# Routing stretch of a hybrid diffusion step: order of router logits, modulation chunks and list product, and who finishes four chunks

## The chip, the cores and the metric

The kernel runs on one core of one Trainium2 chip. The metric is device time in microseconds (us) of one execution; several runs are made and the median is taken. The engines are TensorE (PE), VectorE (DVE), ScalarE (ACT), GpSimd (POOL) and SyncE (SP), which issues most of the transfers. SPq, ACTq and POOLq are the instruction queues of those engines where they issue DMAs or do register work.

## The reference

Two trunk layers; each has a mixing sub-layer (pooling, neighbourhood attention, latent attention) and a channel sub-layer, a hierarchical mixture of experts. 128 context and 512 latent tokens share the weights; they differ in the conditioning vector. What matters here is the modulation and the routing:

```python
def modulation(cvec, w_mod, b_mod):
    m = (jax.nn.silu(cvec) @ w_mod + b_mod)[..., None, :]
    return jnp.split(m, 6, axis=-1)

def ada_norm(x, g, shift, scale):
    return rmsnorm(x, g) * (1.0 + scale) + shift

...
        xp = xp + gt1 * rmsnorm(y, g_post_mix[l])
        h = ada_norm(xp, g_pre_ffn[l], sh2, sc2)
        y = hier_moe(h, w_group_router[l], w_expert_router[l], w_exp_gate[l], w_exp_up[l], w_exp_down[l])
        xp = xp + gt2 * rmsnorm(y, g_post_ffn[l])
...
def hier_moe(h, w_group_router, w_expert_router, w1, w3, w2):
    ...
    gp = jax.nn.softmax((x @ w_group_router).astype(jnp.float32), axis=-1)
    g_w, g_idx = lax.top_k(gp, 1)
    el = (x @ w_expert_router).astype(jnp.float32).reshape(N, N_GROUPS, EXPERTS_PER_GROUP)
    el_g = jnp.take_along_axis(el, g_idx[:, :, None], axis=1)[:, 0]
    top_w, top_i = lax.top_k(jax.nn.softmax(el_g, axis=-1), TOP_K)
    top_w = top_w / jnp.sum(top_w, axis=-1, keepdims=True)
    expert_id = g_idx * EXPERTS_PER_GROUP + top_i
    ...
```

`D_MODEL` is 1024, there are 16 experts with a hidden width of 256, and everything is float32.

## The kernel before, in words

Each engine runs its own instruction stream over a loop of two layers and meets the others at semaphores. The 640 tokens are five tiles of 128. PE writes into three PSUM buffers, `pair0` to `pair2`, in turn: the list `plan_jobs` names every job of the layer in PE's order, and job i takes buffer i mod 3, so it waits until the reader of job i-3 has released it. The end of that list is written out by hand as `TAIL` (line 92).

The steps of `TAIL` are: `y` (output projection of one tile, 64 matmuls), `ht` (the tile of `h2`, the input of the experts, transposed by 8 PE transposes), `lg` (router logits of a tile: 16 matmul records of 128x20), `mod` (one chunk of 512 columns of the modulation: a weight chunk of 2 MB times the two conditioning vectors, 32 matmul records of 2x256), `cnt` (how many tokens before this one chose the same expert) and `list` (the token numbers of each block of 128 expert slots, 20 matmul records of 128x26). Chunks 6 and 7 are this layer's last gate `gt2`; 8 to 11 belong to the next layer's first norm. In this text mod 6 is the chunk with number 6, lg 4 the logits of tile 4.

The weight chunks lie in a ring of six units of 1 MB. A chunk of the modulation takes two, so mod 9 overwrites mod 6, and mod 10 mod 7. SP issues the loads in the order of `plan_chunks`: it waits until PE has read what lies there (line 605 and following), loads the weights, stores the finished rows of the chunk before the last one to `mod_rows` in DRAM (`store_mods`, which waits for `mod_row`), and loads the bias and gain rows `aux`. After mod 11 it waits for `blocks_ready` and for PE's mod 10, reads the expert number of the first block, and issues `w_gate`, `w_up` and `w_down` (lines 637 to 651).

DVE finishes every chunk: `mod_rows_of` (line 1021) adds the bias rows to the PSUM result and multiplies by the gain, two instructions each on 2 partitions by 256 columns. It also runs the routing, a chain of some 65 small instructions from line 1340 to 1414: maxima and one-hots, `chosen` for `cnt`, a wait for the exponentials of ACT (`routed_b`, line 1361), places and slots, `marks_ready` for `list` (line 1403), `blocks_ready` (line 1414). ACT copies each transposed tile out of PSUM, then waits until the rows of mod 6 and 7 are stored, issues the load of the broadcast gate `gb2` from them, and only then computes the two exponentials (lines 936 to 945).

POOL has nothing in this stretch until `list` has been read by DVE into `src_ids`. It then issues the indirect DMAs that gather 128 rows of `h2_rows` for each block of tokens. PE enters the loop over expert blocks with `gathered` (8 transposes), `up` (64 matmul records) and `down`. For the first block these need the gathered rows, the weights, and mod 9 to 11 read out of PSUM.

## Time and profile before

| what | value |
|---|---|
| median of 3 runs | 2143.77 us (2137.72 to 2143.83) |
| profiled execution | 2149.69 us, span 2147.9 us |
| PE busy | 1905.1 us, 89% of the span |
| DVE busy | 775.7 us, 36% |
| ACT busy | 564.6 us, 26% |
| POOL busy | 168.0 us, 8% |
| chain that ended last: PE | 79% |
| mean granted clock of TensorE | 0.949 |

The profile is one execution. Busy times alone do not tell where time can be saved: PE is the bound as a whole, and what the stretch of the change costs is read from PE's gaps there and from who ends them. In the rows of a timeline, the bracket at the end gives the time for which the engine stood idle before the row, and the work whose end released it. A granted clock of 1.00 is 2.4 GHz and 0.50 is 1.2 GHz.

### The profile page before, as it was taken

To read this page: it belongs to the slowest core of one execution; us is meant where nothing else is said; L and a number is where in the kernel's file an instruction comes from. 1 tells how busy PE (TensorE), PEld (TensorE's weight loads), DVE (VectorE), ACT (ScalarE), POOL (GpSimd) and SP (SyncE) were. 2 spreads that over 40 slices of the span, in tenths; PEclk is the share of its full clock that TensorE was granted. 3 is DMA by queue.
4 is the path that set the end of the run, shared out by engine and by line. 5 is a ranking of instruction groups with operands and counts; after the bars stand their busy time and mean duration, and the time that the engine had idled before them with its cause. 6 is when DMAs were issued, how large, how long until landed. Compare 5 with 4: busy or idle time off the path is not lost.

```text
span 2147.9 us, 30625 instructions
## 1 busy us (share of the span) xinstructions
PE 1905.1 (89%) x12556; PEld 1590.1 (74%) x12556; DVE 775.7 (36%) x1426; ACT 564.6 (26%) x909; POOL 168.0 (8%) x192
## 2 busy tenths in 40 slices
PE   3799898999999996999818998989999999979992
PEld 1698555779999884888708975556899998748881
DVE  1421556753222235111062226477423222341113
ACT  1311251652121120111152103526422111201113
POOL 0201510000000000011020033100000000000101
PEclk8799999999999997999958999999999999989996
DMA  9413352211132418999692123121113214389995
GB/s 338 149 62 82 121 168 79 99 59 60 60 99 74 171 70 309 347 351 361 236 312 84 50 63 140 40 79 60 60 60 99 74 64 177 132 299 359 355 342 206
DMA packets 197424, 340.94 MB, mean 159 GB/s; under 512 B 9948, under 2 KB 121964, under 8 KB 196972
## 3 DMA queue, kind: packets, MB, share of 16 engines
q1 hardware_dynamic: 167804, 266.16, 36.0%
q10 hardware_dynamic: 21728, 44.83, 5.9%
q0 software_dynamic: 7776, 28.32, 3.7%
q8 instruction: 85, 1.39, 0.3%
q14 instruction: 31, 0.25, 0.0%
HBM read 309.50 MB, written 41.30 MB: 163 GB/s over the span
## 4 chain that ended last, share of the span: by engine, by line
PE 79%; DVE 8%; DMA 5%; ACT 3%; issue 3%; SPq 1%; ACTq 1%; POOL 1%; POOLq 0%; DVEq 0%
PE pair L1592 70%; PE opair L1592 5%; PE pair L1638 3%; DVE mid L1178 1%; DMA ring<-in_w_mod 1%; DMA r<-mod_rows 1%; DMA r<-h_rows,ids 1%; DVE r L1434 1%; ACT r L959 1%; DVE mid L1190 1%; SPq L533 1%; ACT ysT_r L742 1%; ACTq L735 0%; DMA ysT<-in_mod_aux 0%; DVE mid L1307 0%
## 5 line engine op out<-in xcount | busy, mean ns | idle before, releaser
L1592 PEld LDWEIGHTS pair<-r,ring 128*128 128x128 f32 x2176 | 252.7, 195 | 18.7 <-issue 15.3
L1592 PE MATMUL pair<-r,ring 128*128 128x128 f32 x2176 | 253.2, 278 | 2.6 <-DVE r L1430 2.6
L1592 PE MATMUL pair<-hT_r,mid_r 128*128 128x320 f32 x768 | 237.3, 309 | 0.0
L1592 PE MATMUL pair<-r_r,ring_r 128*128 128x320 f32 x832 | 211.8, 309 | 2.2 <-DVE ring_r L1051 2.2
L1592 PE MATMUL pair<-ring,r 128*128 128x256 f32 (+1 forms) x776 | 204.7, 422 | 6.7 <-DVE r L1280 3.6
L1638 PE MATMUL pair<-cst,mid 128*128 128x128 f32 (+1 forms) x668 | 107.4, 300 | 113.6 <-DVE mid L1070 80.9
L1638 PEld LDWEIGHTS pair<-cst,mid 128*128 128x128 f32 (+1 forms) x668 | 82.0, 152 | 158.4 <-DVE mid L1070 85.0
L1592 PEld LDWEIGHTS pair<-ring,r 128*128 128x128 f32 x776 | 146.6, 191 | 53.2 <-issue 24.4
L1592 PE MATMUL pair<-ysT_r,mid_r 128*128 128x256 f32 (+1 forms) x768 | 170.5, 313 | 17.2 <-issue 17.2
L1592 PE MATMUL pair<-mid_r 128*128 128x320 f32 x576 | 178.9, 311 | 1.6 <-issue 1.6
L1592 PE MATMUL pair<-r_r,mid_r 128*128 128x256 f32 (+2 forms) x576 | 179.3, 311 | 0.0
L1592 PE MATMUL pair<-mid_r,ring_r 128*128 128x320 f32 x576 | 178.0, 309 | 0.0
L1592 PEld LDWEIGHTS pair<-r_r,ring_r 128*128 128x128 f32 x832 | 145.7, 188 | 2.8 <-DVE ring_r L1051 2.8
L1592 PEld LDWEIGHTS pair<-ysT_r,mid_r 128*128 128x128 f32 x768 | 131.9, 194 | 18.0 <-issue 18.0
L1592 PEld LDWEIGHTS pair<-hT_r,mid_r 128*128 128x128 f32 x768 | 144.2, 188 | 0.5 <-issue 0.5
L1276 DVE TENSOR_TENSOR r<-pair,r 128x640 f32<-128x640 f32 x48 | 39.5, 823 | 274.8 <-PE pair L1592 274.8
L1434 DVE TENSOR_TENSOR r<-r,pair 128x256 f32<-128x256 f32 x34 | 14.3, 421 | 343.4 <-ACT r L959 343.4
L1592 PE MATMUL pair<-r 96*128 96x320 f32 (+4 forms) x512 | 122.3, 431 | 6.4 <-issue 6.4
L881 ACT ACTIVATE r<-pair 128x640 f32<-128x640 f32 x48 | 33.8, 703 | 297.5 <-PE pair L1592 297.5
L1550 POOL COPY ids<-src_ids 128x1 uint32 x34 | 6.2, 184 | 1348.3 <-DVE src_ids L1418 529.2
L1592 PEld LDWEIGHTS pair<-r_r,mid_r 128*128 128x128 f32 x576 | 110.5, 192 | 0.0
L1592 PEld LDWEIGHTS pair<-mid_r 128*128 128x128 f32 x576 | 108.1, 188 | 3.0 <-issue 2.6
(247 smaller groups left out, 2919.1 us busy)
## 6 DMA issues: line engine op xcount, KB each, us to landing
ring<-in_w_mod SPq DMA_DIRECT2D x27, 2048.0 KB, 9.5
ring<-in_w_gate SPq DMA_DIRECT2D x34, 1024.0 KB, 7.0
ring<-in_w_up SPq DMA_DIRECT2D x34, 1024.0 KB, 12.2
ring<-in_w_down SPq DMA_DIRECT2D x34, 1024.0 KB, 10.9
ring<-in_w_in SPq DMA_DIRECT2D x24, 1024.0 KB, 7.3
expert_out<-r ACTq DMA_DIRECT2D x34, 512.0 KB, 7.4
ring<-in_w_in SPq DMA_DIRECT2D x8, 2048.0 KB, 13.6
ring<-in_w_branch SPq DMA_DIRECT2D x12, 1024.0 KB, 5.1
```

Of the source, the lines that this page charges most:

```text
L533: sp.dma_start(pro_w[i], w_mod[0, :, i * 512:(i + 1) * 512].rearrange("(k p) n -> p k n", p=P)).then_inc(pro_in[i], 16)
L742: ins = nc.scalar.copy(out, rows)
L881: nc.scalar.activation(sig[:, i % 2, :], ps[:, MID:MID + T], ACT.Sigmoid)\
L959: nc.scalar.activation(sil[:, s, :], pair[1][:, s * 512:s * 512 + FF], ACT.Silu).then_inc(sil_ready, 1)
L1178: V.tensor_tensor_reduce(by_columns(na_probs[i % 3][:, a * w:(a + 1) * w]), by_columns(ps[:, a * 512:a * 512 + w]), bias, -1.0, MOST, ALU. ...
L1190: ins = V.tensor_scalar(own, own, na_inv[i % 2][:, a:a + 1], None, ALU.mult)
L1276: ins = V.tensor_tensor(mergedT[:, m, :] if first else sig[:, i % 2, :], ps[:, MID:MID + T], sig[:, i % 2, :], ALU.mult)
L1434: V.tensor_tensor(hid[:, s, :], sil[:, s, :], pair[1][:, s * 512 + FF:s * 512 + 2 * FF], ALU.mult)\
L1550: G.tensor_copy(src_id[s], src_ids[:, ds(it * 2 + s, 1)]).then_inc(id_ready, 1)
L1592: return nc.tensor.matmul(out, lhsT, rhs, start=first, stop=last, skip_group_check=True)
L1638: last = nc.tensor.transpose(ps[0:s.shape[1], a:a + P], s, ident)
```

## The change

`TAIL` is reordered in two places: lg 4 goes ahead of mod 7, and `list` goes between mod 9 and mod 10. DVE reads the logits of tile t-2 right after the residual sum of tile t, and not at the end of the tile. Mod 6 to 9 are no longer finished by DVE: ACT copies them from PSUM to SBUF (`mod_evicted`), which frees the buffer, and POOL adds the bias and multiplies by the gain (`mod_rows_by_pool`). DVE finishes mod 10 and 11, both after its read of `list`. SP no longer stores rows ahead of a weight load of the modulation; the store behind the load remains. POOL reads the list once the rows of mod 0 to 9 are done.

```diff
-        ("lg", 2), ("ht", 3), ("mod", 6), ("lg", 3), ("ht", 4), ("mod", 7), ("lg", 4), ("mod", 8), ("cnt", 0),
-        ("mod", 9), ("mod", 10), ("list", 0), ("mod", 11)]
+        ("lg", 2), ("ht", 3), ("mod", 6), ("lg", 3), ("ht", 4), ("lg", 4), ("mod", 7), ("mod", 8), ("cnt", 0),
+        ("mod", 9), ("list", 0), ("mod", 10), ("mod", 11)]
...
+        def mod_rows_by_pool(pool, n):
+
+            pool.wait_ge(aux_in[n % 2], 16 * MT * (n // 2 + 1))
...
+            await_read(pool, ("mod", n))
+            for i in range(MT):
+                own = slice(32 * i, 32 * i + 2)
+                ins = nc.gpsimd.tensor_tensor(modst[n][own], modst[n][own], aux[n][own, 0:MW], ALU.add)
+            ins.then_inc(aux_added, 1)
+            pool.wait_ge(aux_added, n - N_IN + 1)
+            for i in range(MT):
+                own = slice(32 * i, 32 * i + 2)
+                nc.gpsimd.tensor_tensor(modst[n][own], modst[n][own], aux[n][own, MW:2 * MW], ALU.mult).then_inc(mod_row, 1)
+
+        def mod_evicted(act, n):
+
+            ps = await_job(act, ("mod", n))
+            if mod_before(n) is not None:
+                await_mod_stored(act, mod_before(n))
+            for i in range(MT):
+                own = slice(32 * i, 32 * i + 2)
+                ins = nc.scalar.copy(modst[n][own], ps[own, 0:MW])
+            ins.then_inc(freed[PAIR_OF[("mod", n)]], 1)
...
-                        if before[0] == "mod":
+                        if before[0] == "mod" and key[0] != "mod":
                             store_mods(before[1])
...
+                mod_evicted(act, N_IN)
                 tail_transposed(TT - 1)
-                await_mod_stored(act, N_IN)
-                await_mod_stored(act, N_IN + 1)
+                for n in range(N_IN + 1, N_IN + 3):
+                    mod_evicted(act, n)
+                for n in range(N_IN, N_IN + 2):
+                    await_mod_stored(act, n)
                 for g in range(2):
                     act.dma_start(gb2[:, g, :], mod_rows[g:g + 1, 5 * D:6 * D].partition_broadcast(P)).then_inc(gb_in, 16)
...
+                for n in range(N_IN + 3, NMOD - 2):
+                    mod_evicted(act, n)
                 act.wait_ge(rows_zeroed, 16 * (NB - spare + 1))
...
                     V.tensor_tensor(x2[:, t, :], x2[:, t, :], yb[:, t % 2, :], ALU.add).then_inc(x2_new, 1)
+                    if t >= 2:
+                        logits(t - 2)
                     inverse_root(t, 2 * t + 2)
...
-                    if t >= 2:
-                        logits(t - 2)
-                mod_rows_of(N_IN)
                 logits(TT - 2)
-                mod_rows_of(N_IN + 1)
                 logits(TT - 1)
...
-                mod_rows_of(N_IN + 2)
...
-                mod_rows_of(N_IN + 3)
-                mod_rows_of(N_IN + 4)
                 ps = await_job(dve, ("list", 0))
...
-                mod_rows_of(N_IN + 5)
+                dve.wait_ge(mod_row, MT * (NMOD - 2))
+                for n in (NMOD - 2, NMOD - 1):
+                    mod_rows_of(dve, V, n)
...
+                for n in range(N_IN, NMOD - 2):
+                    mod_rows_by_pool(pool, n)
+                pool.wait_ge(mod_row, MT * (NMOD - 2))
                 await_read(pool, ("list", 0))
```

On PE, at the end of a layer, from ht 3 to mod 11, the order before is this (`cst,ysT` is `ht`, `router_sb` is `lg`, `ring,cols` is `mod`, `small,cst` is `cnt`, `<-mid 128x26` is `list`):

```order
L1592 MATMUL pair2<-ring,cols 2x256 x16
L1592 MATMUL pair0<-router_sb,mid 128x20 x8
L1638 MATMUL pair1<-cst,ysT 128x128 x8
L1592 MATMUL pair2<-ring,cols 2x256 x16
L1592 MATMUL pair0<-router_sb,mid 128x20 x8
L1592 MATMUL pair1<-ring,cols 2x256 x16
L1592 MATMUL pair2<-small,cst 128x80 x2
L1592 MATMUL pair0<-ring,cols 2x256 x16
L1592 MATMUL pair1<-ring,cols 2x256 x16
L1592 MATMUL pair2<-mid 128x26 x10
L1592 MATMUL pair0<-ring,cols 2x256 x16
```

and now:

```order
L1628 MATMUL pair2<-ring,cols 2x256 x16
L1628 MATMUL pair0<-router_sb,mid 128x20 x8
L1674 MATMUL pair1<-cst,ysT 128x128 x8
L1628 MATMUL pair2<-router_sb,mid 128x20 x8
L1628 MATMUL pair0<-ring,cols 2x256 x16
L1628 MATMUL pair1<-ring,cols 2x256 x16
L1628 MATMUL pair2<-small,cst 128x80 x2
L1628 MATMUL pair0<-ring,cols 2x256 x16
L1628 MATMUL pair1<-mid 128x26 x10
L1628 MATMUL pair2<-ring,cols 2x256 x16
L1628 MATMUL pair0<-ring,cols 2x256 x16
```

Lg 4 has moved ahead of mod 7 and `list` ahead of mod 10; with them the PSUM buffers of lg 4, mod 7, `list` and mod 10 have changed.

On ACT, from the last transposed tiles to the exponentials (`r1<-` and `mid<-pair... 2x256` now are the copies of mod chunks, `hT<-mod_rows` is the load of `gb2`, of which the second row is left out), before:

```order
L915 COPY mid<-pair1 128x1024 [waits filled0,filled1]
L911 DMA h2_rows<-ysT 128x1024 [waits h2_ready]
L915 COPY mid<-pair1 128x1024 [waits filled0,filled1]
L940 DMA hT<-mod_rows 128x1024 [waits mod_stored1,mod_stored0]
L943 ACT_TABLE_LOAD
L943 ACTIVATE small<-small 128x20 [waits routed_a]
L945 ACTIVATE small<-small 128x5 [waits routed_a]
```

and now, with the first of the two copies of each chunk:

```order
L963 COPY mid<-pair1 128x1024 [waits filled0,filled1]
L570 COPY r1<-pair2 2x256 [waits filled2]
L959 DMA h2_rows<-ysT 128x1024 [waits h2_ready]
L963 COPY mid<-pair1 128x1024 [waits filled0,filled1]
L570 COPY mid<-pair0 2x256 [waits filled0]
L570 COPY r1<-pair1 2x256 [waits mod_stored0,filled1]
L991 DMA hT<-mod_rows 128x1024 [waits mod_stored1,mod_stored0]
L994 ACT_TABLE_LOAD
L994 ACTIVATE small<-small 128x20 [waits routed_a]
L996 ACTIVATE small<-small 128x5 [waits routed_a]
L570 COPY mid<-pair0 2x256 [waits mod_stored1,filled0]
```

The copies of mod 6, 7 and 8 now stand ahead of the load of `gb2` and of the exponentials; that of mod 9 stands behind them.

On DVE, from the last instruction of the routing to mod 11, the first of each two, before:

```order
L1414 CAST ids<-small 128x1 [waits dve_step]
L1030 SCALAR_TENSOR_TENSOR mid<-pair0,mid 2x256 [waits mod_stored1,aux_in1,filled0]
L1036 TENSOR_TENSOR mid<-mid 2x256 [waits freed0]
L1030 SCALAR_TENSOR_TENSOR r1<-pair1,mid 2x256 [waits mod_stored0,aux_in0,filled1]
L1036 TENSOR_TENSOR r1<-r1,mid 2x256 [waits freed1]
L1418 CAST src_ids<-pair2 128x26 [waits filled2]
L1030 SCALAR_TENSOR_TENSOR mid<-pair0,mid 2x256 [waits mod_stored1,aux_in1,filled0]
L1036 TENSOR_TENSOR mid<-mid 2x256 [waits freed0]
```

and now:

```order
L1447 CAST ids<-small 128x1 [waits dve_step]
L1449 CAST src_ids<-pair1 128x26 [waits filled1]
L535 SCALAR_TENSOR_TENSOR r1<-pair2,mid 2x256 [waits aux_in0,mod_stored0,filled2,mod_row]
L541 TENSOR_TENSOR r1<-r1,mid 2x256 [waits freed2]
L535 SCALAR_TENSOR_TENSOR mid<-pair0,mid 2x256 [waits mod_stored1,aux_in1,filled0]
L541 TENSOR_TENSOR mid<-mid 2x256 [waits freed0]
```

The read of `list` now directly follows the routing, and mod 10 follows it with a wait for all rows before.

## Rows read from the trace of the kernel before

**Rows 1.** Timeline of PE, both layers (start us, us, what)
```profile
806.69 2.13 PE L1592 MATMUL pair<-router_sb,mid 128*128 128x20 f32 x16 [2.10 <-DVE small L1300]
...
810.54 4.17 PE L1592 MATMUL pair<-ring,cols 128*2 128x256 f32 x32
...
816.53 3.62 PE L1592 MATMUL pair<-ring,cols 128*2 128x256 f32 x32
...
830.76 5.98 PE L1592 MATMUL pair<-ring,cols 128*2 128x256 f32 x32 [4.82 <-DMA ring<-in_w_mod]
836.68 2.41 PE L1592 MATMUL pair<-mid 128*128 128x26 f32 x20
839.02 3.62 PE L1592 MATMUL pair<-ring,cols 128*2 128x256 f32 x32
850.04 1.97 PE L1920 MATMUL pair<-cst,r 128*128 128x128 f32 x8 [7.40 <-DMA r<-h_rows,ids]
853.33 10.33 PE L1592 MATMUL pair<-r,ring 128*128 128x128 f32 x64 [1.32 <-DVE r L1430]
...
868.12 7.31 PE L1592 MATMUL pair<-r,ring 128*128 128x128 f32 x64
...
1917.51 9.07 PE L1592 MATMUL pair<-r,ring 128*128 128x128 f32 x64 [1.32 <-DVE r L1430]
```

**Rows 2.** Chain of waits, the first gather: start, us, what
```profile
841.62 8.38 DMA r<-h_rows,ids
```

**Rows 3.** Timeline of DVE, routing part
```profile
816.85 0.17 DVE L1340 TENSOR_REDUCE small<-small 128x5 f32<-128x20 f32 x1
...
821.43 0.24 DVE L1358 TENSOR_TENSOR small<-small 128x80 f32<-128x80 f32 x1
...
823.39 0.17 DVE L1362 TENSOR_REDUCE small<-small 128x5 f32<-128x20 f32 x1
...
832.26 0.50 DVE L1402 TENSOR_TENSOR mid<-mid,cst 128x130 f32<-128x130 f32 x2
```

**Rows 4.** Timeline of ACT, same stretch
```profile
803.91 1.01 ACT L915 COPY mid<-pair 128x1024 f32<-128x1024 f32 x1 [0.23 <-issue]
...
820.91 0.81 ACTq L940 DMA_DIRECT2D hT<-mod_rows  x2
821.75 1.28 ACT L943 ACT_TABLE_LOAD   x1 [10.10 <-DMA mod_rows<-mid]
```

**Rows 5.** Timeline of SP's queue
```profile
816.52 0.53 SPq L602 DMA_DIRECT2D mod_rows<-mid  x2
...
818.89 0.41 SPq L615 DMA_DIRECT2D ring<-in_w_mod  x1
...
837.34 1.47 SPq L632 DMA_DIRECT2D mid<-in_mod_aux  x2
841.09 0.41 SPq L647 DMA_DIRECT2D ring<-in_w_gate  x1
```

**Rows 6.** DMA issues 800.6 to 801, 841.5 to 842.1: KB each, us to landing
```profile
ring<-in_w_mod SPq DMA_DIRECT2D x1, 2048.0 KB, 14.7
...
ring<-in_w_up SPq DMA_DIRECT2D x1, 1024.0 KB, 10.8
```

**Rows 7.** Groups by line and form, ACT: busy us, mean ns
```profile
L755 ACT COPY r<-pair 128x256 f32<-128x256 f32 x8 | 3.0, 380 | 0.0
```

**Rows 8.** Groups by line and form, POOL
```profile
L1501 POOL TENSOR_TENSOR r_r<-hT,ysT_r 128x512 fp32r<-128x512 f32 x8 | 15.9, 2022 | 0.0
...
L1529 POOL TENSOR_TENSOR u_sb<-ysT,u_sb 128x656 f32<-128x656 f32 x8 | 12.7, 1591 | 0.6
...
L1527 POOL TENSOR_TENSOR ysT<-ysT,cst 128x8 f32<-128x8 f32 x32 | 5.7, 208 | 0.7
```

**Rows 9.** Stretches of 1 us: busy us by engine, PEclk, DMA share, GB/s
```profile
819.00:820.00 1.00, 1.00 (x12) 0.28 (x6) 0.85 (x5) 0.00 (x0) 0.00 (x0) 1.00 0.27 86
...
846.00:847.00 1.00, 0.00 (x0) 0.00 (x0) 0.00 (x0) 0.00 (x0) 0.00 (x0) 0.50 1.11 372
```

More of the change, by code:

```diff
@@ L1019, in link @@
                     dve.wait_ge(dve_step, steps[0])
-                def mod_rows_of(n):
-                    ps = await_job(dve, ("mod", n))
-                    dve.wait_ge(aux_in[n % 2], 16 * MT * (n // 2 + 1))
-                    if mod_before(n) is not None:
-                        await_mod_stored(dve, mod_before(n))
-                    one = 1.0 if MODS[n][0] // 2 in (1, 4) else 0.0
-                    for i in range(MT):
-                        own = slice(32 * i, 32 * i + 2)
-                        ins = V.scalar_tensor_tensor(out=modst[n][own], in0=ps[own, 0:MW], scalar=one, in1=aux[n][own, 0:MW],
-                                                     op0=ALU.add, op1=ALU.add)
-                    ins.then_inc(freed[PAIR_OF[("mod", n)]], 1)
-                    await_read(dve, ("mod", n))
-                    for i in range(MT):
-                        own = slice(32 * i, 32 * i + 2)
-                        V.tensor_tensor(modst[n][own], modst[n][own], aux[n][own, MW:2 * MW], ALU.mult).then_inc(mod_row, 1)
                 def split_low(i):
@@ L1155, in attend_context @@
                     V.tensor_tensor(c_probs, c_probs, by_head(c_inv), ALU.mult).then_inc(c_scaled, 1)
-                    mod_rows_of(n_mod)
+                    mod_rows_of(dve, V, n_mod)
                     await_job(dve, (kind + "c", 1))
@@ L1196, in neighbourhood @@
                         if i == 0:
-                            mod_rows_of(n_mod)
+                            mod_rows_of(dve, V, n_mod)
                             context_values("na", 1)
@@ L1232, in latent @@
                         if i == 0:
-                            mod_rows_of(n_mod)
+                            mod_rows_of(dve, V, n_mod)
                             context_values("ml", 2)
@@ L1237, in latent @@
                         if i == MOD_UNIT:
-                            mod_rows_of(N_ML)
+                            mod_rows_of(dve, V, N_ML)
                         if i % 3 == 2 and i // 3 < KD:
@@ L1266, in _ @@
                 split_low(N_WIN)
-                mod_rows_of(N_ML + 1)
+                mod_rows_of(dve, V, N_ML + 1)
                 await_mod_stored(dve, N_IN - 1)
```

22 lines of the change are left out of this document (added).

## The prediction

> **What bounds the kernel now.** I read the timeline of PE first. The change touches one stretch that occurs once in each of the two layers, from the last output tile to the first expert block, and PE's rows show what closes it. The reader is to see PE's gaps: it waits 2.1 us for DVE before the fourth router tile, 4.82 us for the weights of mod 10, and 7.40 us for the gathered rows before the first expert's transposes; from 853.33 on it runs on with no gap named [rows 1]. So a microsecond won or lost at the start of the first up-projection goes through one to one, and nothing else here counts. In what follows all times are those of the first layer; the second repeats it 1064 us later.
>
> Second, the chain of waits: the gather is issued at 841.62 and lands 8.38 us later [rows 2]. Third, DVE's timeline: routing starts at 816.85, `chs` is ready near 821.7, the part behind `routed_b` starts at 823.39, and the marks for the list product are done near 832.8 [rows 3]. ACT explains 823.39: its exponentials stand behind the load of `gb2`, which waits until the rows of mod 7 are stored; it issues that load at 820.91 and then loads a table for 1.28 us [rows 4]. Fourth, SP's queue: rows of mod 7 stored from 816.52, weights of mod 10 issued at 818.89, the last aux load at 837.34, and the first expert's `w_gate` at 841.09 [rows 5]. The landings of that queue: mod 8's weights 14.7 us after their issue at 800.7, and the first expert's `w_up` 10.8 us after its issue right behind `w_gate`'s, so at 852.4 [rows 6]. The gather path allows the first up-projection at 853.33 and the weights at 852.4: the two ends are within 1 us of each other, and a gain on the gather alone is worth almost nothing.
>
> **The change, part by part.**
>
> *The logits.* Before, lg 3 starts at 806.69, released by DVE's read of lg 2, which stood behind all of h2's work [rows 1]. Now that read comes before. What is late next is ACT's copy of ht 3, done at 804.9 [rows 4]: lg 3 starts near 805.0, ht 4 near 807.0, ACT copies it (1.0 us), lg 4 runs from 809.1 to 811.0. Mod 7 follows, 811.0 to 814.6 (3.62 us as mod 8 took). Routing on DVE then starts at 811.3 instead of 816.85, a lead of 5.6 us, and `chs` is there at 816.1. Mod 8 comes to its weights: 800.7 + 14.7 = 815.4, so it runs 815.4 to 819.0. The count product follows to 819.7 and mod 9 to about 824.5.
>
> *What becomes of the lead.* DVE still stops for `routed_b`, and ACT still issues `gb2` before its exponentials. So the release is the store of mod 7's rows, and these are now made by two engines. ACT: two copies, at 380 ns for 128x256 from PSUM [rows 7], so 0.76 us, ends at 815.4. POOL: four operations of 2x256. The trace has none of that size on POOL. Two-input additions and products there took 208 ns at 8 elements, 1591 ns at 656 (in place, as here) and 2022 ns at 512 in strided fp32r form [rows 8]. The line through the first two gives 0.208 + 248 x 2.13 ns = 0.74 us each; through the first and third 1.10 us each; the dearest bound is a whole 2.0 us each, the cheapest 0.2. I take 0.74, as these are plain in-place f32 rows: 3.0 us for four. Rows of mod 7 are then ready at 818.4 instead of 816.5: 1.9 us later, though PE delivers mod 7 at the same time as before (814.6). The store took from 816.52 to 820.9 before, and the two loads of DMA work in front of it are the same now; I take 821.4, with 820.9 and 822.8 as ends (the same 4.4 us from 818.4). DVE goes on at about 823.9 instead of 823.39. The lead of 5.6 us becomes a wait on DVE of about 7 us, and the 1.7 us of mod 8's rows no longer done by DVE lie in that wait too. The marks are ready at 833.3, 0.5 us later than before.
>
> The Trainium skill speaks against POOL here: GPSIMD Engine Reference, section Key points, says that it shares its SBUF interfaces with VectorE and contends with DVE instructions that have two SBUF inputs. No row here shows POOL and DVE side by side in this stretch. By that rule the rows of mod 8 and 9 could stretch, since DVE then works through its chain, while those of mod 7 fall in DVE's wait and would not; the sum stays as it is.
>
> The Trainium skill, DMA: Bandwidth & Descriptors, section Anatomy of one DMA, puts the fixed cost of a transfer at about 2.0 us. The trace has 4.4 us for the two small stores of mod 7 with issue, which stood behind mod 9's weights. By the page's figure alone the store would be there at 820.9, an estimate, and DVE would be back at its old time.
>
> *SP's queue.* Lifting the wait for rows off the weight loads changes little: for mod 9 to 11 the same rows have been waited for one chunk earlier, before the aux load. So mod 10's weights still stand behind the store of mod 7's rows: 818.89 + 1.9 = 820.8. In that time the DMA engines have nothing: their share fell to 0.27 between 819 and 820 already [rows 9]. Mod 10's weights land 11.8 us after issue (830.7 before [rows 1]), so at 832.6. Nothing waits for them now, since the list product comes first. Mod 11's are issued near 825 and land by 838.
>
> *The list product.* It moves ahead of mod 10: it starts at 833.3 instead of 836.68. But PE has been idle for almost 9 us then. Before, after an idle time of 4.82 us, mod 10 ran 5.98 us instead of 3.62, at the lower clock. The list took 2.41 us at the full clock; 1.2 instead of 2.4 GHz makes at most 4.8. I take 4.7: it ends at 838.0, 1.1 us before its old end at 839.1. Mod 10 then runs 838.0 to 842.0 (3.62 and 0.4 for what is left of the slow clock) instead of ending at 836.7, and mod 11 from 842.0 to 845.6, instead of 842.6.
>
> *What starts the experts.* `w_gate` waits for mod 10's product. Before, that was hidden: the last aux load ended at 838.8 and reading the registers took until 841.09. Now mod 10 ends last, and of those 2.3 us of register work the pair count's share stands ahead of the wait and the expert number's behind it; I take half, 1.1 us: 843.1, 2.0 us later. The gathers get out of the way: POOL has the list 1.1 us earlier, so the first is issued at 840.5, on empty DMA engines. Before, `w_up` landed 11.3 us after `w_gate`'s issue with both gathers (0.5 MB each) mixed in. At the 372 GB/s of that time [rows 9] one gather is 1.4 us. I take one of them out of the way and 9.8 us: `w_up` lands at 852.9. The ends are 8.4 (no gather) and 11.3 (both). The last rows of mod 11 are off DVE at 847.4, the transposes and their copy end at 850: not binding. The first up-projection starts at 852.9 instead of 853.33: 0.4 us less per layer. POOL's work of mod 6 to 9 ends near 828 and hides behind DVE's chain; if that cover were gone, `src_ids` would wait.
>
> *Clock of the first up-projection.* It took 10.33 us in the first layer and 9.07 in the second, against 7.31 when up to speed [rows 1]. PE stood idle for 7.4 us ahead of it, and the granted clock was 0.50 by 846, the lower level of 1.2 GHz [rows 9]. In the new order PE idles about 4 us between its transposes and the weights, after some 2 before them. I expect a loss of the same size, with plus or minus 2 us per layer for it.
>
> Sum: 2 x -0.4 = about -1 us. The profiled run took 2149.69 us (span 2147.9), 5.9 above the median of 2143.77; the sum made against it is 2148.7, and set against the median it is 2142.9. Taking the bounds together (POOL's price, the list at 2.4 to 4.8, the gathers' 1.4 each way, the clock) one layer lies between -3 and +2.5, so this case by itself spans 2137 to 2149.
>
> **The rivals.**
>
> *Faster: the list is not slowed.* If the list product is held by its instructions and not by the clock (2.41), it ends at 835.7, mod 10 at 839.3, `w_gate` goes at 840.4 and `w_up` lands at 850.0; the gather is there before. That is 3.3 us, and if PE's shorter idle keeps the clock up, another 3.0 and 1.76: 2 x 3.3 + 4.8 = 11.4, so 2132. For it: no row has so small a product at the lower clock. Against: mod 10's products, with two columns of weights each, were stretched by it.
>
> *Slower: POOL's hand-over decides.* Each of mod 7's four operations at the dearest bound of 2.0 us makes 8.1 instead of 3.0. Mod 10's weights, the store, the exponentials and so the marks, the list and `w_gate` all move by 5.1: +4.7 us per layer with the 0.4 won taken off, 2 x 4.7 = 9.4, so 2153. From 1.65 us per operation on it is more than 0.3% slower. For it: POOL's prices spread by a factor of 1.7 for similar sizes. Against: the dear ones are strided.
>
> *No change, by the landings.* If the store of mod 7 takes its 4.4 us again (822.8) and both gathers meet `w_gate`, the start is +1.4 +1.5 -0.4 = +2.5 per layer: 2149.
>
> **How the numbers follow.** The likeliest case has 0.60, the faster rival 0.15, the slower 0.12, the landings 0.13. The predicted time is 2142.9. A comparison tells about 0.3% (6.4 us) from no change. The likeliest case leaves 0.02 on each side of that; so faster is 0.15 + 0.02 = 0.17, slower 0.12 + 0.02 = 0.14 with nothing for the landings, same 0.69. The range goes from 2134.5, which leaves out most of the faster rival, to 2149.5, which leaves out the slower.
>
> **What would show it.** Right: DVE's routing starts 5 us or more earlier in relation to the last output tile, and then DVE idles 5 to 8 us until ACT's exponential; POOL's operations of 2x256 take 0.6 to 1.1 us; mod 10's weights are issued about 2 us later; PE's gap before the list is 8 to 9 us and the list takes over 4 us; `w_gate` is issued 1.1 us after mod 10's end, later than before; the first up-projection waits for `w_up` and not for the gather. Wrong: DVE passes `routed_b` with no wait, POOL's operations above 1.65 us, a list of 2.4 us, or a first up-projection in 7.3 us.

## The result and the profile after

The changed kernel takes 2154.97 us (median of 6 runs, 2152.01 to 2157.84); the kernel before took 2143.79 in the runs beside it. The ratio is 1.0053 with an interval of 1.0036 to 1.0070: slower by 11.2 us, some 5.6 per layer. The prediction said 2142.9 and gave slower a chance of 0.14; its range ended at 2149.5. The profiled run took 2155.81 us (span 2154.0), only 6.1 us more than the profiled run before, since single runs of either kernel spread over 6 to 10 us. So totals are read from the timed runs and causes from places inside the stretch. There times are given relative to the start of lg 2 on PE (before 797.57 and 1861.65, after 800.16 and 1862.79), as "rel".

PE's timeline after, as in [rows 1]: start, duration, what, and in brackets the idle time ahead and what ended it.

```profile
807.57 1.96 PE L1628 MATMUL pair<-router_sb,mid 128*128 128x20 f32 x16 [0.39 <-ACT mid L963]
809.38 1.07 PE L1674 MATMUL pair<-cst,ysT 128*128 128x128 f32 x8
811.55 3.47 PE L1628 MATMUL pair<-router_sb,mid 128*128 128x20 f32 x16 [1.10 <-ACT mid L963]
814.95 8.84 PE L1628 MATMUL pair<-ring,cols 128*2 128x256 f32 x64
...
838.69 4.47 PE L1628 MATMUL pair<-mid 128*128 128x26 f32 x20 [10.75 <-DVE mid L1435]
843.09 8.43 PE L1628 MATMUL pair<-ring,cols 128*2 128x256 f32 x64
853.58 1.06 PE L1956 MATMUL pair<-cst,r 128*128 128x128 f32 x8 [2.06 <-issue]
859.16 9.18 PE L1628 MATMUL pair<-r,ring 128*128 128x128 f32 x64 [4.52 <-DMA ring<-in_w_up]
...
1923.87 9.30 PE L1628 MATMUL pair<-r,ring 128*128 128x128 f32 x64 [5.25 <-DMA ring<-in_w_up]
```

Lg 3 starts at rel 7.41 instead of 9.12 and lg 4 at 11.39 instead of 17.07: the new order does what it says. But lg 4 takes 3.47 us where it took 1.96, and the 64 matmuls behind it are mod 7 and mod 8 in 8.84 us, where two chunks at full speed are 7.1. The list waits 10.75 us for the marks. The stretches of PE show why lg 4 and mod 7 are long (columns: stretch, length, busy time of PE, PEld, DVE, ACT, POOL, then PEclk, DMA share and GB/s):

```profile
811.00:812.00 1.00, 0.45 (x3) 0.45 (x3) 0.00 (x0) 0.50 (x1) 0.91 (x2) 0.87 1.04 414
812.00:814.00 2.00, 2.00 (x12) 2.00 (x11) 0.00 (x0) 0.00 (x0) 0.00 (x0) 0.50 1.04 416
814.00:818.00 4.00, 4.00 (x21) 1.91 (x23) 2.53 (x14) 0.00 (x0) 0.00 (x0) 0.50 1.00 363
...
824.00:825.00 1.00, 1.00 (x12) 0.55 (x13) 0.00 (x0) 0.56 (x2) 0.62 (x2) 1.00 0.06 16
825.00:826.00 1.00, 1.00 (x12) 0.42 (x10) 0.00 (x0) 0.00 (x0) 0.94 (x2) 1.00 0.01 4
```

Right behind PE's idle time of 1.10 us ahead of lg 4 the granted clock falls to 0.50 (1.2 of 2.4 GHz) and stays there until past 818. In the second layer lg 4 takes 3.60 us and mod 7 and 8 together 9.92. The last two rows are what [rows 9] showed in small: the DMA engines stand nearly empty, now for some 4 us. Then POOL, ACT, SP's queue and DVE in that order:

```profile
821.26 1.49 POOL L556 TENSOR_TENSOR mid<-mid 2x256 f32<-2x256 f32 x2 [9.27 <-ACT mid L570]
822.83 1.51 POOL L561 TENSOR_TENSOR mid<-mid 2x256 f32<-2x256 f32 x2
```
```profile
820.38 0.73 ACT L570 COPY mid<-pair 2x256 f32<-2x256 f32 x2 [8.88 <-PE pair L1628]
823.83 0.73 ACT L570 COPY r<-pair 2x256 f32<-2x256 f32 x2 [2.72 <-PE pair L1628]
825.84 0.81 ACTq L991 DMA_DIRECT2D hT<-mod_rows  x2
826.69 1.28 ACT L994 ACT_TABLE_LOAD   x1 [2.12 <-DMA mod_rows<-mid]
```
```profile
824.36 0.53 SPq L650 DMA_DIRECT2D mod_rows<-mid  x2
...
826.73 0.41 SPq L663 DMA_DIRECT2D ring<-in_w_mod  x1
...
849.20 0.41 SPq L695 DMA_DIRECT2D ring<-in_w_gate  x1
```
```profile
819.85 0.24 DVE L1392 TENSOR_TENSOR small<-small 128x80 f32<-128x80 f32 x1
828.33 0.17 DVE L1395 TENSOR_REDUCE small<-small 128x5 f32<-128x20 f32 x1 [8.24 <-ACT small L996]
...
831.64 1.62 DVE L1412 SCALAR_TENSOR_TENSOR small<-small 128x16 f32<-128x16 f32 x4
```

ACT has mod 7 at 820.38, POOL finishes its rows at 824.34, they land at 825.84, and only then come the load of `gb2`, the table and the exponentials. DVE had the chosen marks at 820.09 and stood idle for 8.24 us. That is the chain that closes the marks, the list, mod 10 and `w_gate`. Mod 10 runs at the lower clock as well, behind PE's idle time ahead of the list: 5.0 us in the first layer and 5.8 in the second.

### The profile page after: what moved, and what is told of

Read it like the earlier page. It is cut to its first block, busy times and chain, and to the rows that moved or that the text cites. A ratio compares the mean times of both kernels' runs of the same rounds, so it can differ in the third digit from the quotient of the medians.

```text
span 2154.0 us, 30647 instructions
## 1 busy us (share of the span) xinstructions
PE 1909.2 (89%) x12556; PEld 1594.6 (74%) x12556; DVE 763.1 (35%) x1394; ACT 569.9 (26%) x925; POOL 190.8 (9%) x224
## 4 chain that ended last, share of the span: by engine, by line
PE 79%; DVE 9%; DMA 4%; ACT 3%; issue 3%; SPq 1%; ACTq 1%; POOL 1%; DVEq 0%; POOLq 0%
PE pair L1628 70%; PE opair L1628 5%; PE pair L1674 3%; DVE mid L1214 1%; DMA r<-mod_rows 1%; DMA ring<-in_w_up 1%; DVE r L1467 1%; ACT r L1012 1%; ACT ysT_r L790 1%; DVE mid L1226 1%; SPq L581 0%; ACTq L783 0%; DMA ysT<-in_mod_aux 0%; DMA mod_rows<-mid 0%; DVE mid L1255 0%
## 5 line engine op out<-in xcount | busy, mean ns | idle before, releaser
L1628 PEld LDWEIGHTS pair<-r,ring 128*128 128x128 f32 x2176 | 251.9, 194 | 25.5 <-issue 25.5
L1312 DVE TENSOR_TENSOR r<-pair,r 128x640 f32<-128x640 f32 x48 | 39.5, 823 | 274.8 <-PE pair L1628 274.8
L1628 PEld LDWEIGHTS pair<-mid_r,ring_r 128*128 128x128 f32 x576 | 108.2, 188 | 0.0
## 6 DMA issues: line engine op xcount, KB each, us to landing
ring<-in_w_down SPq DMA_DIRECT2D x34, 1024.0 KB, 11.2
```

The lines of the kernel that those rows point to most:

```text
L1312: ins = V.tensor_tensor(mergedT[:, m, :] if first else sig[:, i % 2, :], ps[:, MID:MID + T], sig[:, i % 2, :], ALU.mult)
L1628: return nc.tensor.matmul(out, lhsT, rhs, start=first, stop=last, skip_group_check=True)
```

## The experiments

**Theory 1**: mod 7's rows are late because lg 4 and mod 7 run at the lower clock, and since ACT's exponentials stand behind the landing of those rows, DVE waits and all behind it is late. **Theory 2**: who finishes the rows, that is the hand-over from ACT to POOL and POOL's work beside DVE's. **Theory 3**: the list product ahead of mod 10. Each pair in the table is layer 1 / layer 2 of the profiled run, relative to lg 2; the ratio is of the timed runs to those of the kernel before.

| kernel | ratio (interval) | list | `w_gate` issued | first up |
|---|---|---|---|---|
| before | 1 | 39.1 / 39.6 | 43.5 / 43.5 | 55.8 / 55.9 |
| after | 1.0053 (1.0036 to 1.0070) | 38.5 / 39.2 | 49.0 / 50.5 | 59.0 / 61.1 |
| e1_lg4_behind_mod7 | 1.0021 (1.0009 to 1.0034) | 36.4 / 37.0 | 47.9 / 48.5 | 58.8 / 58.5 |
| e2_list_behind_mod10 | 1.0048 (1.0032 to 1.0065) | 45.3 / 43.2 | 48.1 / 46.1 | 62.2 / 58.7 |
| e3_exp_first | 1.0000 (0.9988 to 1.0012) | 34.7 / 35.6 | 45.7 / 46.7 | 55.5 / 58.0 |
| e6_pe_busy | 1.0028 (1.0017 to 1.0039) | 37.2 / 36.2 | 48.5 / 47.4 | 59.6 / 58.0 |
| e4_dve_finishes | 1.0033 (1.0021 to 1.0045) | 37.1 / 37.4 | 47.4 / 47.9 | 57.3 / 58.4 |
| e8_count_ahead | 0.9997 (0.9984 to 1.0011) | 32.0 / 32.0 | 44.6 / 44.3 | 53.6 / 53.1 |
| e9_weights_ahead | 0.9991 (0.9978 to 1.0003) | 31.5 / 32.1 | 41.8 / 42.5 | 51.9 / 53.7 |
| e10_all_and_busy | 0.9969 (0.9956 to 0.9982) | 29.2 / 29.2 | 39.5 / 37.9 | 50.6 / 51.6 |
| e13_all_dve_finishes | 0.9968 (0.9955 to 0.9980) | 29.5 / 30.8 | 39.7 / 41.1 | 52.3 / 53.4 |
| e11_busy_thrice | 0.9953 (0.9939 to 0.9967) | 29.2 / 31.3 | 38.0 / 40.1 | 50.1 / 51.8 |
| e12_before_weights_ahead | 1.0046 (1.0030 to 1.0061) | 40.7 / 40.3 | 49.0 / 48.6 | 60.5 / 60.0 |
| e15_before_weights_exp | 0.9999 (0.9987 to 1.0011) | 36.9 / 35.3 | 45.2 / 43.5 | 56.6 / 55.0 |
| e14_before_busy | 1.0001 (0.9993 to 1.0010) | 38.2 / 38.0 | 43.3 / 43.6 | 54.6 / 55.0 |
| e5_before_exp_first | 1.0003 (0.9991 to 1.0016) | 38.6 / 37.5 | 43.5 / 43.5 | 55.1 / 54.9 |

The last column carries most of the time: for these 15 kernels the measured difference of the medians lies between 1.5 us below and 4.3 above the sum of its two differences from before. For the changed kernel the sum is 3.2 + 5.2 = 8.4 against 11.2. So a difference of a few us between two totals is not explained by this column.

**e1_lg4_behind_mod7.** Only the table of the tail is edited.

```diff
-("ht", 4), ("lg", 4), ("mod", 7), ("mod", 8)
+("ht", 4), ("mod", 7), ("lg", 4), ("mod", 8)
```

> The changed kernel with lg 4 back behind mod 7 on PE; the list product ahead of mod 10 and the finishing by ACT and POOL stay. Theory 1 (mod 7 comes late, because lg 4 is put ahead of it and both run at the lower clock, and all that ACT's exponentials release is later by it): mod 7 ends 15 to 17 us after the start of lg 2 instead of 20.2, its rows are there near 21 instead of 24.2, DVE's wait for the exponentials shrinks from 8.2 us to 1 or 2, w_gate goes 3 to 4 us earlier per layer, and the time is 2147 to 2149, 3 to 4 us below halfway between the two kernels. Theory 2 (the hand-over from ACT to POOL decides): mod 7's rows still come 3.8 us after its product, and since routing then starts 2 to 3 us later nothing is won: 2153 to 2156. Theory 3 (the list product ahead of mod 10 decides): 2153 or more as well, with w_gate still 1.1 us after mod 10's end and mod 10 behind the list at the lower clock.

Measured 2150.02 us, 6.9 below the changed kernel by the ratios. Mod 7's rows are stored at rel 17.9 instead of 24.2, so it is the place of lg 4 and the clock that made them late. But the list wins only 2.1 us, and the time lies above the 2147 to 2149 expected. ACT's timeline of the first layer shows the second thing that stands ahead of the exponentials, mod 8's copy:

```profile
818.75 0.36 ACT L570 COPY r<-pair 2x256 f32<-2x256 f32 x1 [8.18 <-PE pair L1628]
```

Mod 7's rows were long on their way, but ACT waited 8.18 us for mod 8's product, itself 5.31 us long here, before it came to the load of `gb2`. In the second layer the copy was done first, and the landing of mod 7's rows, 5.2 us after their issue, came last. The exponentials end at rel 25.6 and 25.5. The prediction had neither wait at this length.

**e2_list_behind_mod10.**

```diff
-("mod", 9), ("list", 0), ("mod", 10), ("mod", 11)]
+("mod", 9), ("mod", 10), ("list", 0), ("mod", 11)]
```

> The changed kernel with the list product back behind mod 10; the rest stays. Mod 10's weights land near 838 and the marks near 838.6, so mod 10 would run from 838 to 843 and the list to 845.5. Theory 3 (the order of list and mod 10 is what makes the experts late): w_gate goes at 844 instead of 849.2, the gathers 3 us later than now and mixed with w_gate and w_up (11.3 us to landing), so the first up-projection starts 2 to 4 us earlier per layer and the time is 2147 to 2151. Theories 1 and 2 (mod 7's rows are late): the marks stay at 38.5 us after the start of lg 2, and what w_gate wins the gathers lose: 2153 to 2157.

Measured 2155.70: no change to the changed kernel, so theory 3 falls for this stretch, with the marks as late as they are (no run has this order with early marks). `w_gate` does go 0.9 and 4.5 us earlier, but the transposes wait for the gather instead:

```profile
857.28 1.97 PE L1956 MATMUL pair<-cst,r 128*128 128x128 f32 x8 [7.68 <-DMA r<-h_rows,ids]
```

**e3_exp_first.** Both exponentials are moved ahead of ACT's copy of mod 7; the same four lines are taken out behind the load of `gb2`.

```diff
+                act.wait_ge(routed_a, 1)
+                nc.scalar.activation(e4, e4, ACT.Exp).then_inc(routed_b, 1)
+                act.wait_ge(routed_a, 2)
+                nc.scalar.activation(m2, m2, ACT.Exp).then_inc(routed_b, 1)
                 for n in range(N_IN + 1, N_IN + 3):
                     mod_evicted(act, n)
...
```

> The changed kernel with ACT's two exponentials of the routing put ahead of its copy of mod 7, so ahead of the load of gb2 that waits for mod 7's rows. Theory 1: the lead of routing is lost only in DVE's wait of 8.2 us for these exponentials; without it DVE goes on at once, the marks are ready 6 to 8 us earlier (31 to 32.5 after the start of lg 2 instead of 38.5), the list runs then and nothing slows it; mod 10's weights still land near 838 and w_gate follows mod 10 at 843 to 844 instead of 849.2. The first up-projection starts 5 to 6 us earlier per layer: 2143 to 2146. Theory 2 (SP's queue behind mod 7's rows holds the stretch, by mod 10's weights): the marks come earlier but w_gate wins no more than 2 us, 2150 to 2153.

Measured 2145.34, the time before: this one move of two small instructions takes back all that the change lost. The marks come at 34.7 and not at 32, as DVE's timeline says (its next wait is for the count product, which stands behind mod 8 on PE), and its rows are longer beside POOL's (the four operations of line 1412 took 0.81 us in the kernel before, that of line 1430 took 1.49):

```profile
819.57 0.17 DVE L1404 COPY small<-pair 128x16 f32<-128x16 f32 x1 [4.05 <-PE pair L1628]
...
822.15 1.22 DVE L1412 SCALAR_TENSOR_TENSOR small<-small 128x16 f32<-128x16 f32 x4
...
827.02 2.01 DVE L1430 TENSOR_TENSOR mid<-small,cst 128x1280 f32<-128x1280 f32 x1
```

**e6_pe_busy.**

```diff
+                def kept_busy(count):
+                    for k in range(count):
+                        nc.tensor.transpose(opair[:, k % KD * P:(k % KD + 1) * P], h2[:, TT - 1, k % KD * P:(k % KD + 1) * P], ident)
...
                     steps_of[kind](n)
+                    if (kind, n) == ("ht", TT - 1):
+                        kept_busy(12)
```

> The changed kernel with 12 more transposes (128x128, results never read) on PE right behind ht 4, in the gap of 1.10 us in which it waits for ACT's copy. They take 12 x 0.134 = 1.6 us, so lg 4 starts 0.5 us later. Theory 1a (PE's idle time ahead of lg 4 is what drops the granted clock to 0.50 for 6.6 us): the clock stays at 1.00 or falls for much less, lg 4 takes 1.9 instead of 3.5 us and mod 7 3.6 instead of 5.4, mod 7's rows come 2.8 us earlier and the time is 2148 to 2151. Rival (the clock falls all the same, as it does once in this stretch in the kernel before too, for 2.1 us): lg 4 and mod 7 as long as now, 0.5 us later, 2155 to 2157.

Measured 2150.87, 5.4 below the changed kernel. PE's timeline and a window of it:

```profile
810.78 1.47 PE L1941 MATMUL opair<-cst,ysT 128*128 128x128 f32 x12
812.09 1.92 PE L1628 MATMUL pair<-router_sb,mid 128*128 128x20 f32 x16
813.94 3.62 PE L1628 MATMUL pair<-ring,cols 128*2 128x256 f32 x32
```
```profile
812.00:814.00 2.00, 2.00 (x21) 1.94 (x21) 0.00 (x0) 0.00 (x0) 0.51 (x1) 1.00 1.03 409
```

With the gap filled the clock stays at 1.00, and lg 4 and mod 7 take 1.92 and 3.62 us, in both layers. All runs together say the same: with the gap of 1.10 us ahead of lg 4 the lower clock met lg 4 and mod 7 in all 12 layers (the changed kernel, e2, e3, e4, e8, e9); with the gap filled both were at full speed in all 8 (e6, e10, e11, e13), and so they were in the 2 layers of e1, which has no gap there. That filling this gap takes the lower clock away from lg 4 and mod 7 is shown. ACT has mod 7 at rel 16.95 instead of 20.22 and 21.44: the clock made mod 7 late by 3.3 and 4.5 us. Not all of it is won at the list (1.4 and 3.1 us), since mod 8's copy and the store, both behind weights again, hold ACT as in e1. And 6 us of the loss stay, with mod 7 on time: the list still takes 4.47 us and mod 10 behind it 5.8 and 5.7.

**e4_dve_finishes.** ACT's copies and POOL's four-step rows are taken out of the changed kernel, and DVE makes the rows.

```diff
                 logits(TT - 2)
+                mod_rows_of(dve, V, N_IN)
                 logits(TT - 1)
...
                 V.tensor_tensor(chs, ch1, ch2, ALU.add).then_inc(chosen, 1)
+                mod_rows_of(dve, V, N_IN + 1)
+                mod_rows_of(dve, V, N_IN + 2)
...
+                mod_rows_of(dve, V, N_IN + 3)
                 ps = await_job(dve, ("list", 0))
```

> The changed kernel (lg 4 ahead of mod 7, list product ahead of mod 10) with the rows of mod 6 to 9 finished by DVE again: mod 6 between the reads of lg 3 and lg 4, mod 7 and 8 behind the chosen marks, mod 9 ahead of the read of the list. Theory 2 (the hand-over from ACT to POOL, and POOL beside DVE, cost time): mod 7's rows are there 1.9 us after its product instead of 4, so near 22.1 after the start of lg 2 instead of 24.2 to 25.4; DVE passes the exponentials near 26, its small operations take 0.17 to 0.2 each again, and the list starts near 35.5 instead of 38.5: 2149 to 2151. Theory 1 alone (the lower clock and the order on PE decide, and who finishes the rows does not): within 1 us of the changed kernel, 2154 to 2156.

Measured 2150.35, 4.3 below the changed kernel: theory 2 has a share. The store is issued at rel 23.0 and 23.3 instead of 24.2 and 25.4. In the first layer the exponentials end 0.55 us earlier by it, and the list starts 1.5 us earlier; the other 0.9 us are DVE's, whose small operations are short again with POOL silent (line 1410 here is line 1412 of the changed kernel, 1.62 us there):

```profile
829.96 0.81 DVE L1410 SCALAR_TENSOR_TENSOR small<-small 128x16 f32<-128x16 f32 x4
```

**e8_count_ahead**, on top of e3_exp_first, to remove the 4.05 us:

```diff
-("mod", 7), ("mod", 8), ("cnt", 0),
+("mod", 7), ("cnt", 0), ("mod", 8),
```

> The changed kernel with the exponentials ahead of the copy of mod 7 (as in e3_exp_first) and the count product ahead of mod 8 on PE instead of behind it. In e3_exp_first DVE waited 4.05 us for the count product. If that wait is what is left of the lost lead, the list starts near 31.5 after the start of lg 2 instead of 34.7, and what is late next is mod 10: its weights are issued at 26.6 as before and land near 37.8, so mod 10 ends at 42 and w_gate goes at 43 instead of 45.7: 2140 to 2143. Rival: w_gate and the landings behind it do not follow the list, because SP's queue is held by mod 7's rows; then 2144 to 2146 with the list early and PE idle ahead of mod 10.

Measured 2144.23, above the 2140 to 2143 expected. In the trace the list comes nearly as expected (rel 32.0), `w_gate` 1.3 to 1.6 us later than that (44.6 and 44.3 instead of 43), and the up-projection starts 2.2 and 2.7 us earlier than before, but of those 4.9 us the timed runs show 0.6. This is the largest disagreement of the table, and it stays unexplained.

**e9_weights_ahead**, on top of e8_count_ahead: SP's queue is reordered by one held step.

```diff
...
                     if key[0] == "mod":
-                        n = key[1]
+                        held.append(key[1])
+                        if key[1] == N_IN + 3:
+                            continue
+                    for n in held if key[0] == "mod" else ():
                         j, ahead = MODS[n]
...
```

> As e8_count_ahead, and on SP's queue mod 10's weights go ahead of the store of mod 7's rows and of the aux loads of mod 9, so that they wait only for mod 7's product to free their place in the ring. They are issued near 20.5 after the start of lg 2 instead of 26.6. If the 4 us in which the DMA engines stood nearly empty were a loss on the path, mod 10's weights land near 33 to 34 instead of 37.8, mod 10 runs right behind the list from 36 to 41 and w_gate goes at 41 to 42: 2136 to 2140. Rival (PE at the lower clock behind the list is the limit, weights are early enough anyway): no more than 1 us below e8_count_ahead.

Measured 2142.48, with an interval that still holds 1, so the 2136 to 2140 expected were not reached. Mod 10 now runs right behind the list, `w_gate` goes at rel 41.8 and 42.5, as expected; the up-projection starts 3.9 and 2.2 us earlier than before, and of these 6.1 us the timed runs show 2.4 at most.

**e10_all_and_busy** adds e6's 12 transposes to it.

> As e9_weights_ahead, with the 12 unread transposes of e6_pe_busy between ht 4 and lg 4. Theory 1a (the granted clock stays at 1.00 in lg 4 and mod 7 by them): lg 4 takes 1.9 instead of 3.5 us, routing starts 1.5 us earlier, the list near 30, and w_gate goes 1 to 2 us earlier than in e9_weights_ahead, so 2133 to 2138. Rival: with the list early and PE idle for less time ahead of it, the stretch is bound by mod 10's weights or by the slow clock of list and mod 10, and the transposes win nothing: within 1 us of e9_weights_ahead.

Measured 2137.41, faster than before by 0.31% and than e9 by 5.1 us. The only edit between them is the filled gap:

```profile
804.37 1.47 PE L1946 MATMUL opair<-cst,ysT 128*128 128x128 f32 x12
805.68 1.92 PE L1633 MATMUL pair<-router_sb,mid 128*128 128x20 f32 x16
807.53 3.62 PE L1633 MATMUL pair<-ring,cols 128*2 128x256 f32 x32
```

**e11_busy_thrice** fills two more gaps, behind mod 9 and behind the first transposes of gathered rows.

```diff
+                    if (kind, n) == ("mod", N_IN + 3):
+                        ident_busy(16)
...
                 gathered(0, 0, 0)
+                ident_busy(20)
```

> As e10_all_and_busy, with two more groups of unread transposes on PE: 16 behind mod 9, in the gap ahead of the list product, and 20 behind the first transposes of gathered rows, in the gap ahead of the first up-projection. If PE's idle time ahead of each is what brings the lower clock, the list takes 2.4 us in both layers, mod 10 about 3.7 instead of 5.6, and the first up-projection 7.3 to 7.6 instead of 9.0; that is 1.6 us per layer at the up-projection and 0 to 2 ahead of it: 2131 to 2135. Rival: the first up-projection is slow for another reason (weights and rows that still arrive), the clock stays low there, and the time stays at 2136 to 2139.

Measured 2135.22, 0.47% below the kernel before and the best of both kernels and all experiments. List, mod 10 and up-projection of the first layer:

```profile
827.44 2.41 PE L1633 MATMUL pair<-mid 128*128 128x26 f32 x20 [0.53 <-DVE mid L1440]
829.78 5.31 PE L1633 MATMUL pair<-ring,cols 128*2 128x256 f32 x32
...
848.32 7.31 PE L1633 MATMUL pair<-r,ring 128*128 128x128 f32 x64
```

List and up-projection are at full speed there (4.47 and 9.18 in the changed kernel). Mod 10 is not, against the expectation of 3.7 us: 5.31 and 5.29. In the second layer the up-projection took 10.15 us all the same, since PE stood idle for 3.47 us between the last of the 20 transposes and the landing of `w_up`. There the lower clock also met ht 4 and the 12 transposes ahead of lg 4 (2.76 us instead of 1.47), while PE was busy, so lg 4 came 1.6 us later.

**e13_all_dve_finishes** is e10_all_and_busy with DVE making the rows.

> As e10_all_and_busy, with the rows of mod 6 to 9 finished by DVE: mod 6 between the reads of lg 3 and lg 4, mod 7 behind the chosen marks, mod 8 and 9 behind the marks for the list. Theory 2 in a stretch without the stalls: DVE gives 1.7 us to mod 7's rows and gets about as much back, since POOL no longer slows its small operations, so the list starts within 0.7 us of 29.2, and the time is 2136 to 2139, as with ACT and POOL. If the finishing by ACT and POOL is a loss in any order: 2135 or less. If it is a gain once the stalls are gone: 2140 or more.

Measured 2139.57, its ratio to the kernel before within 0.0001 of that of e10: with the stalls gone the timed runs show no difference between the two ways to finish the chunks (each interval reaches about 0.0013 to either side, 2.7 us).

**e12_before_weights_ahead** makes e9's edit on SP in the kernel before.

> The kernel before, in its old order and with DVE finishing all rows, and only this changed on SP's queue: mod 10's weights go ahead of the store of mod 7's rows and the aux loads of mod 9. They are issued near 17.2 after the start of lg 2 instead of 21.3, so mod 10 no longer stands between the marks (35.2) and the list (39.1): the list starts near 35.3 and the gather is issued 3.5 us earlier. w_gate stays at 43.5, held by the last store, the last aux load and the reading of registers; w_up lands 1 to 2 us earlier with one gather out of the way. 2140 to 2142. If the new order on PE is what gives e9_weights_ahead its time, this one stays at 2143 to 2145.

Measured 2155.92, slower by 0.46%, where a gain was expected. The mechanism is the change's own. ACT, then DVE:

```profile
826.67 1.13 ACTq L945 DMA_DIRECT2D hT<-mod_rows  x2
827.84 1.28 ACT L948 ACT_TABLE_LOAD   x1 [14.70 <-DMA mod_rows<-r]
```
```profile
829.48 0.17 DVE L1367 TENSOR_REDUCE small<-small 128x5 f32<-128x20 f32 x1 [3.86 <-ACT small L950]
```

Mod 7's rows were issued at 818.80 behind 2 MB of weights and landed by 826.67, 7.9 us later (9.3 in the second layer); the exponentials waited for that. In the first layer the lower clock also made these rows 1.6 us later than before; in the second they were issued at the old time, and the list started 0.7 us later than before all the same.

**e15_before_weights_exp** moves the exponentials ahead in it, as e3 does.

> As e12_before_weights_ahead (the kernel before, mod 10's weights ahead of the store of mod 7's rows on SP's queue), with ACT's two exponentials ahead of the wait for mod 7's rows and the load of gb2. If the loss of e12_before_weights_ahead is the exponentials' wait for a store that lands 7.9 us after its issue behind 2 MB of weights, it goes entirely: DVE passes them with no wait, the marks are ready near 35 after the start of lg 2 instead of 40.7, and with mod 10 done before them the list starts at 35.3. DVE reads it behind the rows of mod 9 and 10, near 40.6 instead of 41.6, so no more than 1 us per layer is won on the kernel before: 2141 to 2145. If the weights disturb in another way (DVE slower beside them, mod 8's rows late), 2148 or more.

Measured 2144.88: the whole loss of 0.46% goes. DVE comes to the same instruction with no idle time ahead of it:

```profile
825.92 0.17 DVE L1367 TENSOR_REDUCE small<-small 128x5 f32<-128x20 f32 x1
```

With e3 this is the second pair that differs in nothing but the place of the exponentials.

**e5_before_exp_first** does the same in the kernel before alone.

> The kernel before with ACT's two exponentials ahead of the wait for mod 7's rows and the load of gb2, and nothing else. DVE passed them there without idle time (its row at 823.39 follows the rows of mod 8, which end at 823.32), so their place is worth nothing: within 0.1% of the kernel before, 2143 to 2146. If DVE's order of rows and gates hid a wait after all: up to 1.5 us less per layer, 2141.

Measured 2145.96, no change. Where DVE is not ahead, their place is worth nothing.

**e14_before_busy** fills the gap ahead of lg 3 in the kernel before.

> The kernel before with 14 unread transposes (128x128, of the constant identity) on PE behind mod 6, in the gap of 2.10 us ahead of lg 3. There the granted clock fell to 0.50 for 2.1 us. Theory 1a: it stays at 1.00; lg 3, ht 4 and mod 7 take 1.96, 1.07 and 3.62 us instead of 2.13, 1.95 and 4.17, so lg 4 starts 1.6 us earlier, and all behind it, since mod 7's product also frees the place of mod 10's weights: 2140 to 2142. Rival (the clock falls by its own there, or what is won is hidden behind mod 10's weights): 2144 to 2146.

Measured 2144.52, no change, as the rival case of the expectation said.

```profile
797.21 5.31 PE L1592 MATMUL pair<-ring,cols 128*2 128x256 f32 x32 [0.62 <-DVE mid L1307]
802.45 1.75 PE L1905 MATMUL opair<-cst 128*128 128x128 f32 x14
...
1862.19 5.31 PE L1592 MATMUL pair<-ring,cols 128*2 128x256 f32 x32
```

In the first layer lg 3, ht 4 and mod 7 were at full speed, but mod 6 took 5.31 us instead of 3.62, and lg 4 started only 0.6 us earlier. Mod 6 runs ahead of the transposes, so they did not cause that; it was as slow in one layer each of e2, e4 and e13. In the second layer mod 7 was the slow one (the last row), though PE had stood idle for only 0.43 us ahead of lg 3. So here the lower clock does not hang on the filled gap alone, and what else brings it is open. The kernel before had it for about 3.4 us of its first layer (0.64, 0.50, 0.50 and 0.66 in the four stretches of 1 us from 808), not for the 2.1 of the expectation.

## Why the prediction was wrong

**The step that failed** is in the paragraph on the logits: "Mod 7 follows, 811.0 to 814.6 (3.62 us as mod 8 took)", and with it the next one's "though PE delivers mod 7 at the same time as before". Lg 4 and mod 7 ran at the lower clock, and mod 7 ended at rel 20.2 and 21.4 instead of 17.1. The prediction had noted the lower clock for the list and mod 10, but worked out no price for the one that it found nearest: mod 7's own 4.17 us in [rows 1] instead of 3.62, a sign that the clock had fallen in this very place before. e6 shows the mechanism, and also that it is about half of the loss and not all of it: with mod 7 on time 5.4 of the 11.2 us are gone. By the traces the rest lies in two more terms. The exponentials' wait was set at an end of 823.9 and had no margin (e3, which takes them out of that wait, wins back all 11.2 us). And mod 10 behind the list was given 4.0 us and took 5.0 and 5.8 at the lower clock.

Term by term:

- Lg 3 and lg 4: predicted 805.0 and 809.1, which is rel 7.4 and 11.5; measured 7.41 and 11.39. Right.
- ACT and POOL: predicted 0.76 + 3.0 us; measured 0.73 + 3.08 with 0.15 between. Right, and so is nearly the difference to DVE's way, 2.2 us where 1.9 was predicted. The rows came 5.2 and 6.4 us late, not 1.9, and the rest is the clock: 3.0 and 4.2.
- The store: 4.4 us predicted, 1.5 measured. The DMA engines were nearly empty when it came. So `routed_b` was late by 2.4 and 3.6 us, not by the 5.2 and 6.4 of the rows; predicted 0.5.
- DVE beside POOL: not priced in the sum, 0.9 us in the first layer (four operations 1.62 instead of 0.81 us, one 0.30 instead of 0.17). The prediction looked for the contention in POOL's rows of mod 8 and 9; these took their 1.5 us for each two, and DVE's became longer.
- Marks: +0.5 predicted, +3.3 and +4.0 measured. The list: 4.7 predicted, 4.47 measured.
- Mod 10: 4.0 predicted, near 5.0 and 5.8 measured; `w_gate` 1.05 us behind its end (1.1 predicted), so +5.5 and +7.0 instead of +2.0.
- `w_up` lands 9.7 us after `w_gate`'s issue, 10.3 in the second layer (9.8 predicted), and the up-projection waits for it, not for the gather. Right. Its start is +3.2 and +5.2 instead of -0.4, and the 3.6 us of error in the first layer are the 3.5 of `w_gate`: 2.8 by the marks, 1.0 by mod 10, less 0.2 by the list.

The prediction's core, that the lead of DVE would be lost in its wait for the exponentials, held: 8.24 us of idle time against "about 7" predicted (its own times, 816.1 and 823.9, make it 7.8). It read that as harmless, because the wait's end was set 0.5 us from its old place. An end set by three other engines and a transfer had no bound on the late side except POOL's price and a store of 4.4 us.

**The rivals.** "POOL's hand-over decides" named the right chain and nearly the right time (2153), but that is luck: its price was 0.75 us per operation, far below the 1.65 from which it would decide. "The list is not slowed" fell (4.47 us). "By the landings" fell: the store landed early and the gathers were out of the way, 4.4 and 5.1 us each.

**What is shown and what is not.** Shown: the exponentials' place behind mod 7's landing is what turns any lateness of these rows into lost time (e3, e15, e12, e5); the rows are late by PE's clock (e6, e1) and by the hand-over, and POOL's work makes DVE's own longer (e4). The shares by the ratios, 5.4 us for the clock and 4.3 for the finishing, cannot be added up, since both feed one wait. Not settled: why e8's 4.9 us in the trace are 0.6 in the timed runs (and e9's 6.1 are 2.4); why mod 10 behind the list stays at the lower clock in e11; and what brings the lower clock where no gap stands directly ahead of it (e11 and e14, second layers).

## What to carry to other kernels

When an engine gains time on the others, look up what it next waits for and price everything queued ahead of that on the releasing engine: here a bulk load with a wait for a landing, a wait for another product, and a table load stood ahead of two instructions of 0.2 us. Put short work that others wait for ahead of waits that nobody needs soon. And when work on PE is moved together, work out the time of what follows the idle time left ahead of it at both levels of the clock.

## What the runs showed of the hardware

- The same store of mod 7's rows (two of 2 KB) landed 1.5 us after its issue on nearly empty DMA engines (the changed kernel, both layers), 4.4 and 3.7 behind one chunk of weights (the kernel before) and 7.9 and 9.3 behind more (e12). The Trainium skill, DMA: Bandwidth & Descriptors, section Anatomy of one DMA, puts the fixed part of a transfer issued by POOL at about 2.0 us; this one is issued by SP, and for it the 1.5 us measured here decide, a little below.
- POOL takes 0.75 us for an addition or product of 2x256 f32, in place, where DVE takes 0.42 to 0.43. Beside them DVE's operation on 128x1280 took 2.01 us instead of 1.49 (e3), and one with a single SBUF input (L1410) 0.30 instead of 0.17, while those that read PSUM (L1407, L1408) stayed at 0.17. POOL's became longer too: its two additions of mod 6, beside DVE's operations on 128x1024, took 2.12 us and not 1.49. The Trainium skill, GPSIMD Engine Reference, section Key points, names contention with DVE instructions in a 2-port perf mode or with two SBUF inputs. For two inputs the trace agrees (L1412 and L1430); whether L1410 runs in such a mode no run here shows.
- PE idle for 1.10 us ahead of lg 4 was followed by 6.8 us at 0.50 of the clock in the first layer of the changed kernel. 12 unread transposes in the gap kept it at 1.00 through lg 4 and mod 7 in both layers of e6 and of e10. In the kernel before the clock was at 0.50 for about 3.4 us of the first layer, and with its gap filled (e14) it was so again, in mod 6 in the one layer and in mod 7 in the other, there with PE busy.
